# Delta rule on features-on-partitions convolution outputs: norm factors moved onto decay columns, values, state and output norm

## The reference, cut to what matters

```python
qkv = silu(causal_depthwise_conv(concat([gq, gk_, gv]), gdn_conv_w))
cq, ck, cv = split(qkv)
q = l2norm(cq) * 128 ** -0.5          # l2norm: x * rsqrt(sum(x*x) + eps), per token and head
k = l2norm(ck)
beta = sigmoid(gb); g = -exp(a_log) * softplus(ga + dt_bias)
lower = strict(beta_i * (k_i . k_j) * decay_ij)            # decay from the running sum of g
u, w  = solve(I + lower, [beta * v, beta * exp(gc) * k])
a_qk  = (q_i . k_j) * decay_ij
# per chunk: delta = u - w S;  o = exp(gc) q S + a_qk delta;  S = g_end S + k_dec^T delta
o = rmsnorm(o, gdn_norm_g) * silu(gz)
```

## Time and profile before

| | |
|---|---|
| Time, median of 3 | 1251.29 us (1251.26 to 1252.18) |
| Profiled execution | 1251.01 us, span 1249.8 us |
| PE, DVE, ACT, POOL busy | 1240.9 (99%), 814.7 (65%), 691.5 (55%), 140.7 (11%) us |
| L403, L404, L405, weights on xs | 928 records each, 390 to 400 ns shown for one |
| Load of 128x128 weights (PEld, L403 to L405) | 188 to 189 ns shown for one |
| Weight DMAs of 512 KB | 3.3 to 4.4 us from issue to landing |
| Granted TensorE clock, all 40 slices | 9 (90% or more of full speed) |

### The profile page before, as it was taken

One profiled execution on the slowest core, in us unless ns is written; L12 is line 12 of the kernel. 1 busy time (PEld: TensorE's weight loads), 2 busy tenths in 40 slices (PEclk: granted clock), 3 DMA queues, 4 the chain that ended last, 5 costly groups with the idle time before them and its releaser, 6 DMA issues.

```text
span 1249.8 us, 17456 instructions
## 1 busy us (share of the span) xinstructions
PE 1240.9 (99%) x7066; PEld 1032.7 (83%) x7066; DVE 814.7 (65%) x1114; ACT 691.5 (55%) x1046; POOL 140.7 (11%) x119
## 2 busy tenths in 40 slices
PE   9999999999999999999999999999999999999997
PEld 7888888888888888888888887888888888888886
DVE  5657755566788556655567878746875765755654
ACT  6665644443778645444447765556855364655543
POOL 1130000000231200000000332000320000211112
PEclk9999999999999999999999999999999999999999
DMA  8755466865454657655545534333456543565652
GB/s 299 230 155 185 149 222 202 267 187 163 151 164 160 215 156 250 195 178 180 177 153 186 184 120 150 122 104 101 136 197 240 170 151 126 168 218 174 205 171 85
DMA packets 127697, 220.18 MB, mean 176 GB/s; under 512 B 8336, under 2 KB 71184, under 8 KB 127616
## 3 DMA queue, kind: packets, MB, share of 16 engines
q1 hardware_dynamic: 123360, 205.95, 51.1%
q0 software_dynamic: 2672, 10.20, 2.4%
q10 hardware_dynamic: 1584, 2.92, 0.6%
HBM read 215.88 MB, written 3.15 MB: 175 GB/s over the span
## 4 chain that ended last, share of the span: by engine, by line
PE 96%; issue 1%; DMA 1%; ACT 1%; DVE 0%; POOL 0%; ACTq 0%; SPq 0%; POOLq 0%
PE ps L403 25%; PE ps L405 25%; PE ps L404 25%; PE ps L503 5%; PE ps L507 2%; PE ps L823 1%; PE ps L420 1%; PE ps L680 1%; PE ps L811 1%; PE ps L1076 1%; PE ps L1061 1%; PE ps L782 0%; DMA ar<-in_mem 0%; PE ps L610 0%; DMA raw<-in_w_gate_up 0%
## 5 line engine op out<-in xcount | busy, mean ns | idle before, releaser
L1618 DVE TENSOR_TENSOR spl<-raw,spl 128x1024 fp32r<-128x1024 f32 x387 | 476.7, 1256 | 100.4 <-ACT spl L1109 99.0
L1109 ACT CAST spl<-raw 128x1024 fp32r<-128x1024 f32 x387 | 400.1, 1050 | 177.4 <-PE ps L405 88.3
L403 PE MATMUL ps<-spl,xs 128*128 128x512 f32 x928 | 371.5, 400 | 0.0
L405 PE MATMUL ps<-spl,xs 128*128 128x512 f32 x928 | 362.4, 391 | 0.0
L404 PE MATMUL ps<-spl,xs 128*128 128x512 f32 x928 | 361.8, 390 | 0.0
L405 PEld LDWEIGHTS ps<-spl,xs 128*128 128x128 f32 x928 | 174.3, 188 | 37.1
L403 PEld LDWEIGHTS ps<-spl,xs 128*128 128x128 f32 x928 | 174.5, 188 | 35.6 <-issue 1.5
L404 PEld LDWEIGHTS ps<-spl,xs 128*128 128x128 f32 x928 | 174.7, 188 | 34.1 <-issue 0.5
L403 PE MATMUL ps<-spl,ys 128*128 128x512 f32 x496 | 198.5, 400 | 0.1
L405 PE MATMUL ps<-spl,ys 128*128 128x512 f32 x496 | 193.7, 391 | 0.0
L404 PE MATMUL ps<-spl,ys 128*128 128x512 f32 x496 | 193.4, 390 | 0.0
(11 more groups left out here) (329 smaller groups left out, 1152.2 us busy)
## 6 DMA issues: line engine op xcount, KB each, us to landing
raw<-in_w_in SPq DMA_DIRECT2D x112, 512.0 KB, 3.9
raw<-in_w_gate_up SPq DMA_DIRECT2D x176, 256.0 KB, 4.0
raw<-in_mlp_w SPq DMA_DIRECT2D x64, 512.0 KB, 4.4
raw<-in_w_down SPq DMA_DIRECT2D x44, 512.0 KB, 4.4
raw<-in_w_out SPq DMA_DIRECT2D x24, 512.0 KB, 4.2
raw<-in_xattn_wk SPq DMA_DIRECT2D x8, 512.0 KB, 3.9
raw<-in_xattn_wv SPq DMA_DIRECT2D x8, 512.0 KB, 4.4
raw<-in_w_branch_gdn SPq DMA_DIRECT2D x8, 512.0 KB, 3.3
```

Source lines behind the costliest of these rows:

```text
L403: self.do.matmul(bank, xh, hi, start=start, stop=False)
L405: m = self.do.matmul(bank, xl, hi, start=False, stop=stop)
L1109: self.do.copy(self.k.spl[:, u % NH, 0, :], self.k.raw[:, u % NR, :]).then_inc(*self.up("hi", (u,)))
L1618: self.do.tensor_tensor(lo, self.k.raw[:, u % NR, :], hi.bitcast(F32), ALU.subtract).then_inc(*self.up("lo", (u,)))
```

## The change

q is no longer turned back to tokens and k and q are not scaled and turned again: the Gram, delta and cross products read the convolution outputs y1 and y0 directly. What the scaling did is done elsewhere: k's factor squared and beta go onto the decay's columns (`cg`), the values are multiplied by `ci` = m r on GpSimd (`gdn_rv`), `ckd` carries the factor for the state, and q's factor goes into the output norm (`gdn_out_rs`, `gdn_out`). The sum of squares of q is made by a Square on ScalarE and matmuls with a column of ones (`gdn_queries`). Step numbers of the flows, places of `take` and `give`, and the order of taking lqT and lkT change with it. The core of the diff:

```diff
 class Tensor:
-    def gdn_turn(self, hf, t, i):
-        tmp = self.s2(f"gt{t}")[:, i, :]
...
-            m = self.do.transpose(b[:, h * P:(h + 1) * P], tmp[:, h * P:(h + 1) * P], self.ident())
+    def gdn_queries(self, hf):
+        q, one = h4(self.s(f"qq{hf}")), self.small("one", 32)[:, 0:1]
+        b = self.hold("qs", hf)
+        self.wait_ge(*self.at("pm", "one"))
+        self.wait_ge(*self.at("sq", "qq", hf))
+        for t in range(2):
+            for h in range(4):
+                m = self.do.matmul(b[:, 4 * t + h:4 * t + h + 1], q[:, h, t * P:(t + 1) * P], one, start=True, stop=True)
...
     def gdn_gram(self, hf, t):
-        lq = self.s(f"lq{hf}{t}")
+        q, k = (h4(self.s(f"y{z}{hf}"))[:, :, t * P:(t + 1) * P] for z in range(2))
...
-                m = self.do.matmul(b[:, i * 256:(i + 1) * 256], lq[:, h * 256:h * 256 + P],
-                                   lq[:, h * 256:(h + 1) * 256], start=True, stop=True)
+                self.do.matmul(b[:, i * 256:i * 256 + P], k[:, h], k[:, h], start=True, stop=True)
+                m = self.do.matmul(b[:, i * 256 + P:(i + 1) * 256], k[:, h], q[:, h], start=True, stop=True)
 class Scalar:
-        self.do.copy(lq[:, :, i, :], self.psg(4, "gt", hf, t, i)).then_inc(*self.up("am", ("gt", hf, t, i)))
+    def gdn_queries(self, hf):
+        self.wait_ge(*self.at("dm", "cm", 0, hf, 1))
+        self.fresh(f"qq{hf}")
+        self.do.activation(self.s(f"qq{hf}"), self.s(f"y0{hf}"), ACT.Square).then_inc(*self.up("sq", ("qq", hf)))
 class Vector:
-    def gdn_scale(self, hf, t, i):
...
+    def gdn_queries(self, hf):
+        self.wait_ge(*self.at("mx", "qs", hf))
+        self.do.tensor_scalar(self.small(f"mq{hf}", 8), self.ps("qs", hf)[:, 0:8], 0.25, EPS, ALU.mult,
+                              ALU.add).then_inc(*self.up("dm", ("qs", hf)))
+    def gdn_out_rs(self, hf):
...
+        self.do.tensor_scalar(cq, self.small(f"rq{hf}", 8), 0.25 * P ** -0.5, None, ALU.mult).then_inc(*self.up("dm", ("c0", hf)))
+        self.do.scalar_tensor_tensor(c2, cq, 16.0 / P, cq, ALU.mult, ALU.mult).then_inc(*self.up("dm", ("c1", hf)))
...
+        self.do.tensor_tensor(ss, ss, c2, ALU.mult).then_inc(*self.up("dm", ("gs", hf)))
+        self.do.tensor_scalar(self.small("m" + str(("go", hf)), 8), ss, 16.0 * EPS, None, ALU.add).then_inc(*self.up("ss", (("go", hf),)))
 class Gpsimd:
+    def gdn_rv(self, hf):
+        v = heads(self.s(f"b2{hf}"), P)
+        self.wait_ge(*self.at("dm", "ci", hf))
+        self.wait_ge(*self.at("am", "cb", 2, hf, 1))
+        self.do.tensor_tensor(v, v, bc(self.small(f"ci{hf}", 8), P), ALU.mult).then_inc(*self.up("pm", ("rv", hf)))
 def conv(E, z, hf):
+    if not z:
+        E.take(f"qq{hf}")
+        E.gdn_queries(hf)
+        E.give(f"qq{hf}", ("mx", "qs", hf))
+        yield
+        return
     E.conv_back(z, hf)
+    if z == 2:
+        E.gdn_rv(hf)
 def order(E):
-         (conv(E, 0, 0), (3, 5, 7, 8, 10, 11, 12)), (conv(E, 1, 0), (8, 10, 12, 13, 15, 15, 16)),
-         (gdn_mid(E, 0), (13, 17, 18, 19, 21, 22, 23, 24, 26, 28, 30, 32, 33, 35, 37, 38, 40, 41, 42, 43, 44)),
-         (gdn_mid(E, 1), (30, 32, 33, 34, 36, 37, 38, 39, 40, *range(41, 53))),
-         (conv(E, 0, 1), (14, 16, 20, 20, 22, 24, 25)), (conv(E, 1, 1), (20, 25, 26, 27, 28, 29, 30)),
+         (conv(E, 0, 0), (3, 5, 7, 8, 11)), (conv(E, 1, 0), (8, 10, 12, 13, 15, 15, 16)),
+         (gdn_mid(E, 0), (13, 17, 18, 21, 22, 24, 26, 28, 30, 32, 33, 35, 37, 38, 40, 41, 42, 43, 44)),
+         (gdn_mid(E, 1), (30, 32, 33, 36, 37, 39, 40, *range(41, 53))),
+         (conv(E, 0, 1), (14, 16, 20, 20, 24)), (conv(E, 1, 1), (20, 25, 26, 27, 28, 29, 30)),
```

More of the change, by code:

```diff
@@ L792, in gdn_decay @@
             self.let(("gd", hf, t), "am", "gd", hf, t)
-    def gdn_turn(self, hf, t, i):
-        tmp = self.s2(f"gt{t}")[:, i, :]
-        b = self.hold("gt", hf, t, i)
-        self.wait_ge(*self.at("dm", "gt", hf, t, i))
-        for h in range(4):
-            m = self.do.transpose(b[:, h * P:(h + 1) * P], tmp[:, h * P:(h + 1) * P], self.ident())
-        m.then_inc(*self.up("mx", ("gt", hf, t, i)))
-        self.let(("gt", hf, t, i), "am", "gt", hf, t, i)
+    def gdn_queries(self, hf):
[6 more added lines that the diff above has]
+                m = self.do.matmul(b[:, 4 * t + h:4 * t + h + 1], q[:, h, t * P:(t + 1) * P], one, start=True, stop=True)
+        m.then_inc(*self.up("mx", ("qs", hf)))
+        self.let(("qs", hf), "dm", "qs", hf)
     def gdn_gram(self, hf, t):
-        lq = self.s(f"lq{hf}{t}")
+        q, k = (h4(self.s(f"y{z}{hf}"))[:, :, t * P:(t + 1) * P] for z in range(2))
+        for z in range(2):
+            self.wait_ge(*self.at("dm", "cm", z, hf, 1))
         for hp in range(2):
@@ L912, in gdn_delta @@
     def gdn_delta(self, hf):
-        lq, S = self.s(f"lq{hf}1"), self.s2(f"St{hf}")[:, 1, :]
-        for w, mark in (("sd", "dm"), ("sx", "am")):
+        S = self.s2(f"St{hf}")[:, 1, :]
+        for w, z, mark in (("sd", 1, "dm"), ("sx", 0, "am")):
+            y = h4(self.s(f"y{z}{hf}"))
             b = self.hold(w, hf)
@@ L917, in gdn_delta @@
             for h in range(4):
-                hh, c = slice(h * P, (h + 1) * P), h * 256 + (P if w == "sx" else 0)
-                m = self.do.matmul(b[:, hh], lq[:, c:c + P], S[:, hh], start=True, stop=True)
+                hh = slice(h * P, (h + 1) * P)
+                m = self.do.matmul(b[:, hh], y[:, h, P:2 * P], S[:, hh], start=True, stop=True)
             m.then_inc(*self.up("mx", (w, hf)))
@@ L1911, in gdn_coefs @@
         hs = slice(4 * hf, 4 * hf + 4)
-        rq, rk = th(self.small(f"r{('cq', 0, hf)}", 8)), th(self.small(f"r{('cq', 1, hf)}", 8))
+        rk, mk = (th(self.small(f"{n}{('cq', 1, hf)}", 8)) for n in "rm")
         ex = self.small("ex", 32)
@@ L1915, in gdn_coefs @@
         be = th(self.small("beta", 16))[:, :, hs]
-        c = {n: th(self.small(f"{n}{hf}", 8)) for n in ("cq", "ck", "ckb", "ckd")}
-        self.wait_ge(*self.at("rs", ("cq", 0, hf)))
-        self.do.tensor_scalar(c["cq"], rq, 0.25 * P ** -0.5, None, ALU.mult).then_inc(*self.up("dm", ("c0", hf)))
+        c = {n: th(self.small(f"{n}{hf}", 8)) for n in ("ck", "cg", "ckd", "ci")}
         self.wait_ge(*self.at("rs", ("cq", 1, hf)))
-        self.do.tensor_scalar(c["ck"], rk, 0.5, None, ALU.mult).then_inc(*self.up("dm", ("c2", hf)))
+        self.do.scalar_tensor_tensor(c["ck"], rk, 0.25, rk, ALU.mult, ALU.mult).then_inc(*self.up("dm", ("c2", hf)))
@@ L1921, in gdn_coefs @@
         self.wait_ge(*self.at("dm", "c2", hf))
         self.wait_ge(*self.at("dm", "be"))
[L1923 removed]
+        self.do.tensor_tensor(c["cg"], c["ck"], be, ALU.mult).then_inc(*self.up("dm", ("c3", hf)))
+        self.do.scalar_tensor_tensor(c["ci"], mk, 2.0, rk, ALU.mult, ALU.mult).then_inc(*self.up("dm", ("ci", hf)))
         self.wait_ge(*self.at("dm", "c3", hf))
         self.wait_ge(*self.at("am", "gs"))
[L1926 removed]
+        self.do.tensor_tensor(c["ckd"], c["cg"], ekd, ALU.mult).then_inc(*self.up("dm", ("c4", hf)))
@@ new lines, in gdn_out_rs @@
+    def gdn_out_rs(self, hf):
+        ss, cq, c2 = (self.small(f"{n}{hf}", 8) for n in ("go", "cq", "c2"))
+        self.wait_ge(*self.at("rs", "mq", hf))
+        self.do.tensor_scalar(cq, self.small(f"rq{hf}", 8), 0.25 * P ** -0.5, None, ALU.mult).then_inc(*self.up("dm", ("c0", hf)))
+        self.wait_ge(*self.at("dm", "c0", hf))
+        self.do.scalar_tensor_tensor(c2, cq, 16.0 / P, cq, ALU.mult, ALU.mult).then_inc(*self.up("dm", ("c1", hf)))
+        self.wait_ge(*self.at("sq", ("go", hf)))
+        self.do.tensor_reduce(ss, heads(self.s("q_" + str(("go", hf))), P), AX.X,
+                              ALU.add).then_inc(*self.up("ss", ("r", ("go", hf))))
+        self.wait_ge(*self.at("ss", "r", ("go", hf)))
+        self.wait_ge(*self.at("dm", "c1", hf))
+        self.do.tensor_tensor(ss, ss, c2, ALU.mult).then_inc(*self.up("dm", ("gs", hf)))
+        self.wait_ge(*self.at("dm", "gs", hf))
+        self.do.tensor_scalar(self.small("m" + str(("go", hf)), 8), ss, 16.0 * EPS, None, ALU.add).then_inc(*self.up("ss", (("go", hf),)))
@@ L1990, in gdn_delta @@
         self.wait_ge(*self.at("mx", "sd", hf))
-        self.wait_ge(*self.at("am", "cb", 2, hf, 1))
+        self.wait_ge(*self.at("pm", "rv", hf))
         self.wait_ge(*self.at("dm", "cf", hf))
@@ L2012, in gdn_out @@
     def gdn_out(self, hf):
-        v = self.s(f"ho{hf}")
+        v, r = self.s(f"ho{hf}"), self.small(f"r{('go', hf)}", 8)
         self.wait_ge(*self.at("rs", ("go", hf)))
+        self.do.tensor_tensor(r, r, self.small(f"cq{hf}", 8), ALU.mult).then_inc(*self.up("dm", ("gr", hf)))
+        self.wait_ge(*self.at("dm", "gr", hf))
         self.do.tensor_tensor(heads(v, P), heads(v, P), bc(self.small(f"r{('go', hf)}", 8), P),
@@ L2238, in gdn_decay, with gdn_queries @@
             self.wait_ge(*self.at("pm", "gd0", hf, t))
-            self.wait_ge(*self.at("dm", "be"))
```

(33 more changed lines are left out.)

14 lines of the change are left out of this document (1 added, 13 removed).

## The result

The changed kernel takes 1254.35 us, median of 9 executions (1253.25 to 1255.99). The kernel before took 1251.49 us beside it, also over 9 (1250.80 to 1252.20). The ratio is 1.0024, with a 95% interval of 1.0014 to 1.0034: 2.9 us slower. The forecast was 1251.7 and its range ended at 1253.2. The profiled execution after took 1253.99 us, 2.98 more than the one before.

What follows compares the result with a forecast made beforehand. TensorE, busy 99% of the span, was taken as the bound. Its work at -1.65 us plus a new wait of 2.1 us gave +0.45: 1251.7 us against the median, range 1249.2 to 1253.2.

Steps and rivals of the forecast that it cites:

- The wait is 2.1 us.: First half, flow step 11: TensorE's query matmuls wait for ScalarE's Square of y0; +2.1 us, bounds 0 and 3.1.
- Nothing gives it back: Said of the first half's 2.1 us wait: TensorE's stream stands behind it and has no other idle time.
- Transposes, -5.3 us: TensorE: 48 transposes removed from conv_back and gdn_turn over both halves, at 0.111 us each, save 5.3 us.
- Gram groups, 1.78 us each: TensorE: 8 matmuls of 128 columns replace 4 of 256, 1.78 against 1.72 us, four times: +0.24 us.
- One-column matmuls, 1.7 us a half: gdn_queries on TensorE: 16 records a half at 0.105 us, paced by weight loads; 3.4 us together.
- -1.65 in all: TensorE's work without the wait: -5.3 transposes, +0.24 Gram, +3.4 one-column matmuls, sum -1.65 us.
- the upper bound: gdn_queries: at most 0.111 us a one-column record, the price with 128 columns; 3.6 us for both halves.
- The rival of cheap narrow matmuls: gdn_queries: one-column matmuls cost by their moving columns, 0.3 us for both groups; 1248.6 us, chance 0.06.
- Second half, no wait: Step 24: ScalarE's Square ends with 0.5 us of slack for the query matmuls; wait 0, at most 0.2 us.
- the rival with two waits: Both halves' query matmuls wait behind ScalarE's casts, 2.1 us each: +2.55 us, 1253.9 us, chance 0.12.
- The rival without a wait: No wait at the first query matmuls, ScalarE having less queued than read: 1249.6 us, chance 0.22.
- Beside other work: VectorE, ScalarE and GpSimd changes, decay, output norm and the gate matrix's later slot: each priced at 0.

Runs made afterwards that it cites:

- e6_apart: e1_step13, but TensorE still waits for the Square at step 11, the one-column matmuls coming two steps later without a wait; 1253.08 us, ratio 1.0007.
- e2_wait_only: The kernel before with one wait added: TensorE waits at step 11 for ScalarE's Square of q (first half); 1254.39 us, ratio 1.0019.
- e1_step13: The changed kernel with the first half's query stage (Square and one-column matmuls) at flow step 13 in place of 11; 1250.61 us, ratio 0.9988.
- e4_twice: e1_step13 with each one-column matmul issued twice; 1260.05 us, ratio 1.0059.
- e7_long_wait: e2_wait_only with the wait on a tanh that ScalarE does later; 1257.19 us, ratio 1.0040.
- e5_square_first: The changed kernel with only the first half's Square moved on ScalarE, to step 10 ahead of conv(1, 0); 1250.32 us, ratio 0.9991.
- e8_bf16: e1_step13 with q's squares and the column of ones in bfloat16; 1248.43 us, ratio 0.9967.
- e3_half_wait: The changed kernel with only the first half's Square moved, to the end of step 10 on ScalarE behind the conv work; 1252.66 us, ratio 1.0006.

## Why the prediction was wrong

**The step that failed: "The wait is 2.1 us."** As a wait it was right: the Square was forecast to end at 692.05 and ended at 691.98, the first matmul to start at about 692.3 and started at 692.03, and the wait cost 1.93 us. As the price of the new wait it was mis-sized, because the sum took the clock behind it as given. With the 1.8 us of one-column matmuls that follow directly, the wait brought the granted clock to half and made the products behind it 1.6 us slower. The term is 3.5 us, not 2.1. e6_apart shows that the pair, at these lengths, must stand together, e2_wait_only and e1_step13 that neither does it alone, e4_twice and e7_long_wait that more of either does. "Nothing gives it back" was written of the wait; that the engine would go on at the old pace was never asked, since every stretch read before stood at 1.00. For the stretch of the delta rule the forecast was +0.45 us and the measurement +2.07; the difference is the clock's 1.6, for the wait came out 0.17 cheaper than forecast and the one-column matmuls 0.17 dearer. The other 0.8 us of the miss stand at L1064 and are left open below.

**Transposes, -5.3 us, with +0.24 for the Gram groups: right.** In e1_step13, without a wait, the stretch of the delta rule is 1.48 us shorter although it holds 3.58 us of one-column matmuls; the rest is then -5.06, as forecast. By their medians the two versions without a wait, e1_step13 and e5_square_first, are 1.1 and 1.7 us faster than the kernel before; TensorE's work was forecast at -1.65 in all.

**Gram groups, 1.78 us each: right.** In the kernel after, the group in TensorE's timeline that answers to the earlier trace rows:

```profile
731.13 0.39 PE L405 MATMUL ps<-spl,xs 128*128 128x512 f32 x1
731.35 0.38 PE L813 MATMUL ps<-ar 128*128 128x128 f32 x2
...
733.37 0.39 PE L404 MATMUL ps<-spl,xs 128*128 128x512 f32 x1
```

733.37 - 731.13 - 0.456 = 1.78.

**One-column matmuls, 1.7 us a half: right, 1.78 and 1.79.** The loads set the pace; the timeline of TensorE's weight loads after answers to the earlier trace rows:

```profile
692.03 1.86 PEld L801 LDWEIGHTS ps<-sml,ar 128*128 128x128 f32 x16 [2.10 <-ACT ar L1382]
```

A record takes 0.112 us whether 128 columns move or one; the upper bound was the better value. The rival of cheap narrow matmuls falls. The floor of 25 ns that the Trainium skill gives ("TensorE: Matmul & The Clock Gate", "Back-to-back issue gap") does not set the pace for this operand in full precision: a record takes over four times as long. In bfloat16 (e8_bf16) a record takes 0.04 us, far nearer to it.

**Second half, no wait: right**, so the rival with two waits falls, though its 1253.9 was nearest to what was measured: the mechanism that made the time slower was not among those forecast. The rival without a wait, 1249.6, describes e1_step13 and e5_square_first (1250.6 and 1250.3).

**Beside other work: right.** GpSimd's multiplication of the values took 1.92 us (forecast 2.84) and nothing waits for it; no wait stands at the gate matrix.

**Left open.** TensorE waited 0.7 us at L1064 for ScalarE (L1532) in the execution profiled after, and not before. Other kernels show it as it comes: 0.8 in e3_half_wait, 0.7 in e5_square_first, 0.4 in e1_step13, 0.2 in e2_wait_only and e8_bf16, none in e4_twice, e6_apart and e7_long_wait. It was put down to no part of the change. In the profiled executions it makes 0.8 of the 2.9 us, and whether it does so in the medians is not known. Also open are the 0.6 us by which e2_wait_only lost more than its gap: in its trace the stretch of the delta rule is 2.08 us longer, as the gap says, so they lie outside it or in other executions.

## What to carry to other kernels

On a bound TensorE a wait can cost more than its length. About 2 us of waiting with full products behind it cost just that here; a wait of 3.8 us cost 2.4 more. Where matmuls of few columns stand right behind it, add the products' lost time at half clock, or put producer and consumer two steps later, or the producer ahead of the casts on its own engine: either took the wait and the fall away here. Price a full-precision matmul of few columns by its two weight loads (0.11 us each), and see whether its operands can be bfloat16 (0.31 us in place of 1.79).

## What the runs showed of the hardware that was not expected

The busy share of TensorE did not tell how its clock would be granted. In e4_twice it was 100% busy, without a gap, and the clock went from 1.00 to 0.62 and 0.50 during and behind 3.6 us of one-column matmuls; in e5_square_first it fell behind 3.6 us of other small matmuls. In e2_wait_only it stood idle for 1.78 us and kept 1.00; in e7_long_wait it stood for 3.24 us and fell to 0.50. In the kernel after, a wait of 1.68 us and 1.8 us of such matmuls did it together. The Trainium skill, "TensorE: Matmul & The Clock Gate", section "HAM oscillation — how this bites in real kernels", ties the fallen clock to gaps between matmuls in which TensorE waits: the fall of e7_long_wait behind its wait of 3.24 us agrees with that, and e4_twice shows a fall without any gap.
